# A hybrid encoder block on one core: branch B's values as the stationary operand, and the places around the expert loop rearranged

## The reference, cut to what matters

```python
# branch B: 8 heads of 64, ONE k and ONE v for all heads, k_sel = 128 chosen keys per query
sc = jnp.einsum('bqhd,bqkd->bhqk', q_blk, k_g) * scale - slopes * dist
p = jax.nn.softmax(sc, axis=-1)
y_b = jnp.einsum('bhqk,bqkd->bqhd', p, v_g)
...
merged = g_a * (y_a @ w_branch_a[l]) + g_b * (y_b @ w_branch_b[l])
h = h + merged @ w_out[l]
h = h + memory_cross_attention(rms_norm(h), rms_norm(mem), ...)
...
# experts, E = 32, for the tokens routed to e
hb = silu(xb @ w1[e]) * (xb @ w3[e])      # 1024 -> 512
y += (hb @ w2[e]) * gate                  # 512 -> 1024
...
return rms_norm(h, final_norm)
```

## Time and profile before

| | us |
|---|---|
| three runs | 1073.96, 1075.09, 1076.91 |
| median | 1075.09 |
| the profiled run's own time | 1074.56 |
| its span | 1072.7 |
| PE / DVE / ACT busy in it | 997.1 / 510.8 / 316.6 |

### The profile page before, as it was taken

The page is one execution under the profiler, slowest core; times in us unless marked ns, Lnnn a source line. Parts: engine busy times, 40 slices in busy tenths (PEclk is TensorE's granted clock), DMA queues, the critical chain, the costliest instruction groups (busy, mean ns, idle before and its releaser), DMA issues.

```text
span 1072.7 us, 12319 instructions
## 1 busy us (share of the span) xinstructions
PE 997.1 (93%) x4817; PEld 632.1 (59%) x4817; DVE 510.8 (48%) x923; ACT 316.6 (30%) x589; POOL 38.5 (4%) x58
## 2 busy tenths in 40 slices
PE   5999989999999999999995799999999899899894
PEld 4778857777888888887785344344333333333342
DVE  5269899766437545533337333333333232333335
ACT  6342346665553344443322111111111110001013
POOL 1000000000000000000000100000000000000000
PEclk9999989999999999999997799999999999999997
DMA  7422311212132425521388699999999999999992
GB/s 213 146 79 79 117 41 49 70 40 71 48 118 86 150 83 183 166 79 39 116 322 338 241 427 425 427 427 429 425 425 425 431 424 427 426 427 428 428 384 80
DMA packets 63917, 261.21 MB, mean 244 GB/s; under 512 B 11201, under 2 KB 38898, under 8 KB 49778
## 3 DMA queue, kind: packets, MB, share of 16 engines
q1 hardware_dynamic: 59442, 248.60, 58.5%
q0 software_dynamic: 3104, 7.35, 1.9%
q10 hardware_dynamic: 1312, 4.46, 1.1%
HBM read 260.12 MB, written 4.19 MB: 246 GB/s over the span
## 4 chain that ended last, share of the span: by engine, by line
PE 75%; DMA 13%; DVE 8%; issue 2%; ACT 2%; DVEq 0%; ACTq 0%; POOLq 0%
PE ps L1875 16%; DMA eraw<-in_w 12%; PE ps L1586 12%; PE ps L1588 11%; PE ps L1587 11%; PE ps L1901 8%; PE ps L1912 2%; PE ps L1776 2%; PE ps L1913 2%; PE ps L1755 2%; PE ps L1804 1%; PE ps L1826 1%; PE ps L1763 1%; DVE work L1210 1%; DVE wlo L1175 1%
## 5 line engine op out<-in xcount | busy, mean ns | idle before, releaser
L1875 PE MATMUL ps<-eraw,XT 128*64 128x512 f32 x1024 | 235.8, 604 | 12.5 <-DMA eraw<-in_w 11.7
L1875 PEld LDWEIGHTS ps<-eraw,XT 128*64 128x64 f32 x1024 | 70.5, 138 | 139.6 <-issue 135.7
L1175 DVE TENSOR_TENSOR wlo<-raw,whi 128x2048 fp32r<-128x2048 f32 (+2 forms) x43 | 95.9, 2231 | 108.6 <-ACT whi L879 108.4
L1901 PE MATMUL ps<-eraw,HT 128*64 128x512 f32 x512 | 113.0, 593 | 8.8 <-issue 7.8
L1461 DVE TENSOR_TENSOR h<-ps,h 128x512 f32<-128x512 f32 x128 | 79.4, 683 | 83.4 <-PE ps L1913 83.4
L1586 PE MATMUL ps<-xT_hi,whi 128*128 128x512 f32 (+1 forms) x256 | 104.9, 410 | 3.0 <-DVE xT_lo L1182 2.0
L1587 PE MATMUL ps<-xT_lo,whi 128*128 128x512 f32 (+1 forms) x256 | 101.0, 394 | 0.0
L1588 PE MATMUL ps<-xT_hi,wlo 128*128 128x512 f32 (+1 forms) x256 | 100.8, 394 | 0.0
L879 ACT ACTIVATE whi<-raw 128x2048 fp32r<-128x2048 f32 (+2 forms) x43 | 80.2, 1866 | 45.2 <-PE ps L1588 43.9
L1901 PEld LDWEIGHTS ps<-eraw,HT 128*64 128x64 f32 x512 | 39.9, 137 | 80.1 <-issue 80.1
L1026 ACT ACTIVATE HT<-ps 128x512 f32<-128x512 f32 x16 | 9.6, 598 | 215.5 <-PE ps L1886 215.5
(11 more groups left out here) (304 smaller groups left out, 1539.8 us busy)
## 6 DMA issues: line engine op xcount, KB each, us to landing
eraw<-in_w SPq DMA_DIRECT2D x82, 2048.0 KB, 28.9
eraw<-in_w SPq DMA_DIRECT2D x28, 1024.0 KB, 11.6
raw<-in_w_in SPq DMA_DIRECT2D x9, 1024.0 KB, 5.3
raw<-in_w_gate SPq DMA_DIRECT2D x8, 1024.0 KB, 5.7
raw<-in_w_ckv SPq DMA_DIRECT2D x8, 1024.0 KB, 5.7
raw<-in_w_out SPq DMA_DIRECT2D x4, 1024.0 KB, 5.2
raw<-in_w_cq SPq DMA_DIRECT2D x4, 1024.0 KB, 5.1
raw<-in_w_co SPq DMA_DIRECT2D x4, 1024.0 KB, 5.0
```

Source lines behind the costliest of these rows:

```text
L1175: dve.tensor_tensor(wlo[n % 2][:, 0:w], raw[n % RING][:, 0:w], whi[n % 2][:, 0:w].bitcast(f32), ALU.subtract).then_inc(w_lo, 1)
L1875: ins = pe.matmul(ps[1 + c // 2][rows, :], XT[p % 2][:, kk, rows], eraw[slot][:, first + 512 * k:first + 512 * k + 512], start=(kk == 0), ...
L1901: ins = pe.matmul(ps[4 + n][rows, :], HT[:, ff, rows], eraw[slot][:, first + D * f + 512 * n:first + D * f + 512 * n + 512], start=(ff == ...
```

## The change

- **Branch B.** The roles are exchanged: `vb` (64 columns) is stationary and `pT` (128 columns) moves, the two heads of a unit lie side by side in the two halves of the array, and the result is y transposed. `yb`, its multiplication and the 16 transposes are gone. ACT multiplies the exponentials by the inverted sums ahead of `tr` (two operations a unit), and copies each unit's result to `ybT_hi`; DVE makes `ybT_lo` of it, which now lies in the upper half of h's place. So `h` is loaded behind `mrow`, after the last merge.
- **Around the routing.** `co 3` stands ahead of `hn 1`, and `fT 2`, `fT 3` and `logits 1` ahead of `hn 2`. PE multiplies a constant 3 times behind `rank` and 9 times behind `x_at`, into a bank that nobody reads (`stay_awake`). SP fills the last ring place only when the first gather has landed.
- **The end.** The read of `n_over` stands ahead of each engine's work for the last pair, and ACT's spare root, which brings in the table with roots, behind the branch for `n_over`.

```diff
-    ybT_lo = at("ybT_lo", [P, 4, SEQ], f32r, R_C, 24 * KB)
+    ybT_lo = at("ybT_lo", [P, 4, SEQ], f32r, R_H, 8 * KB)
...
-    yb = at("yb", [P, TT, 512], f32, R_H, 8 * KB)
...
-    steps += [("yT", "b", j) for j in range(4)] + [("split", CH_G[-1] + 2)] + [("sigmoid", i) for i in range(KT // 2)]
+    steps += [("split", CH_G[-1] + 2)] + [("sigmoid", i) for i in range(KT // 2)]
...
-    steps += [("co", 0), ("co", 1), ("fT", 0), ("hn", 0), ("co", 2), ("fT", 1), ("hn", 1), ("co", 3), ("logits", 0),
-              ("hn", 2), ("fT", 2), ("fT", 3), ("logits", 1), ("hn", 3), ("logits", 2), ("logits", 3)]
+    steps += [("co", 0), ("co", 1), ("fT", 0), ("hn", 0), ("co", 2), ("fT", 1), ("co", 3), ("hn", 1), ("logits", 0),
+              ("fT", 2), ("fT", 3), ("logits", 1), ("hn", 2), ("hn", 3), ("logits", 2), ("logits", 3)]
...
             sp.wait_ge(xf_stored, 16 * TT)
+            sp.wait_ge(blk_loaded, 16)
             load_place(NS - 1)
...
-            b, n = use[("yT", "b", 3)]
-            pool.wait_ge(bank_free[b], n + 1)
-            pool.dma_start(h[:, :, :], x[0].rearrange("(t p) n -> p t n", p=P)).then_inc(h_loaded, 16)
             pool.wait_ge(mg_low, len(MERGES))
             pool.dma_start(mrow[:, :, :], mem[0].rearrange("(t p) n -> p t n", p=P)).then_inc(mem_loaded, 16)
+            pool.dma_start(h[:, :, :], x[0].rearrange("(t p) n -> p t n", p=P)).then_inc(h_loaded, 16)
...
+                elif kind == "fin" and UNITS[s[1]][0] == "B":
+                    u = s[1]
+                    qt = UNITS[u][1]
+                    act.wait_ge(sum_inverted, u - len(A_UNITS) + 1)
+                    for m in (0, 1):
+                        b = sbuf[u % 3][m][:, 0:kv(qt)]
+                        ins = act.activation(b, b, ACT.Copy, scale=rsum[:, u % 3, m:m + 1])
+                    ins.then_inc(fin_done, 1)
...
+                    else:
+                        act.activation(ybT_hi[:, j, P * qt:P * qt + P], tile_of(*s)[:, 0:P], ACT.Copy).then_inc(act_hi, 1)
...
-                else:
-
-                    act.activation(sqr[:, 15:16], ident[:, 0:1], ACT.Sqrt)
+            n_over = act.value_load(over_i[0:1, 0:1], min_val=0, max_val=MAX_OVER)
             hidden(NPAIR - 1)
             output(NPAIR - 1)
-            n_over = act.value_load(over_i[0:1, 0:1], min_val=0, max_val=MAX_OVER)
...
+            act.activation(sqr[:, 15:16], ident[:, 0:1], ACT.Sqrt)
...
-                        dve.tensor_tensor(yb[:, qt, P * j:P * j + P].rearrange("p (m n) -> p m n", m=2), p,
-                                          rsum[:, u % 3, 0:2].unsqueeze(2).to_broadcast([P, 2, DH_B]),
-                                          ALU.mult).then_inc(freed(*s), 1)
+                        c = slice(P * qt, P * qt + P)
+                        dve.wait_ge(act_hi, T_NO[s])
+                        dve.tensor_tensor(ybT_lo[:, j, c], tile_of(*s)[:, 0:P], ybT_hi[:, j, c].bitcast(f32),
+                                          ALU.subtract).then_inc(freed(*s), 1)
...
+            n_over = dve.value_load(over_i[0:1, 0:1], min_val=0, max_val=MAX_OVER)
             rest(NPAIR - 1)
-            n_over = dve.value_load(over_i[0:1, 0:1], min_val=0, max_val=MAX_OVER)
...
+            def stay_awake(n):
+
+                for _ in range(n):
+                    pe.matmul(ps[IDLE_BANK][:, 0:256], ident[:, :], gain_o[:, 0:256], start=True, stop=True)
...
+                            for m in (0, 1):
+                                ins = pe.matmul(o[DH_B * m:DH_B * m + DH_B, 0:P], vb[:, k, :], pT[u % 2][m][:, k, :],
+                                                start=(k == 0), stop=(k == qt))
...
-                            for jj in range(4):
-                                copied("yT", "ab"[m], jj)
+                            for jj in range(4 * (1 - m)):
+                                copied("yT", "a", jj)
+                            if m:
+                                copied("av", len(UNITS) - 1)
...
+                    pe.wait_ge(bank_free[IDLE_BANK], bank_uses[IDLE_BANK])
+                    stay_awake(3)
...
                     pair_table(o[:, 0:NE // 2], one_lane, slice(0, P), (by_p, by_tile)).then_inc(full(*s), 1)
+                    stay_awake(9)
```

More of the change, by code:

```diff
@@ L482, in build @@
     max_done, exp_done, fin_done = sem("max_done"), sem("exp_done"), sem("fin_done")
+    sum_inverted = sem("sum_inverted")
     sig_done, mg_sum, mg_high, mg_low = sem("sig_done"), sem("mg_sum"), sem("mg_high"), sem("mg_low")
@@ L516, in build @@
     for s in steps:
-        if s[0] in ("xT", "yT", "mT", "cT"):
+        if s[0] in ("xT", "yT", "mT", "cT") or s[0] == "av" and UNITS[s[1]][0] == "B":
             T_NO[s] = len(T_NO) + 1
@@ L889, in _ @@
                 elif kind == "yT":
[L890 to L893, removed]
-                    else:
-                        act.activation(ybT_hi[:, j, :], p[:, :], ACT.Copy).then_inc(act_hi, 1)
+                    j = s[2]
+                    act.activation(yaT_hi[:, j, :], tile_of(*s)[:, :], ACT.Copy, scale=cols[:, 40:41]).then_inc(act_hi, 1)
                 elif kind == "fT":
@@ L980, in _ @@
                     for g in (2 * s[1], KT + 2 * s[1]):
+                        copied("fm", CH_G[g // 2], 1)
                         v = gates[:, g:g + 2, :].rearrange("p g n -> p (g n)")
@@ L1184, in _ @@
                 elif kind == "yT":
-                    br, j = s[1:]
+                    j = s[2]
                     dve.wait_ge(act_hi, T_NO[s])
[L1187 to L1192, removed]
+                    dve.scalar_tensor_tensor(yaT_lo[:, j, :], tile_of(*s)[:, :], cols[:, 40:41],
+                                             yaT_hi[:, j, :].bitcast(f32), ALU.mult, ALU.subtract).then_inc(freed(*s), 1)
                 elif kind == "index":
@@ L1244, in _ @@
                     else:
-                        dve.reciprocal(rsum[:, u % 3, 0:2], ssum[:, u % 3, 0:2]).then_inc(fin_done, 1)
-                        dve.wait_ge(fin_done, u + 1)
+                        dve.reciprocal(rsum[:, u % 3, 0:2], ssum[:, u % 3, 0:2]).then_inc(sum_inverted, 1)
                 elif kind == "av":
@@ L1599, in pair_table @@
                 return ins
+            IDLE_BANK = [b for b in range(8) if b not in [use[k][0] for k in (("logits",), ("rank",), ("x_at",))]][0]
+            def stay_awake(n):
+                for _ in range(n):
+                    pe.matmul(ps[IDLE_BANK][:, 0:256], ident[:, :], gain_o[:, 0:256], start=True, stop=True)
             for s in steps:
@@ L1645, in _ @@
                 elif kind == "yT":
-                    br, j = s[1:]
-                    if s == ("yT", "b", 0):
-                        copied("av", len(UNITS) - 1)
+                    j = s[2]
                     if s == ("yT", "a", 0):
@@ L1652, in _ @@
                     for t in range(TT):
-                        ins = pe.transpose(o[:, P * t:P * t + P], (ya if br == "a" else yb)[:, t, P * j:P * j + P], ident[:, :])
+                        ins = pe.transpose(o[:, P * t:P * t + P], ya[:, t, P * j:P * j + P], ident[:, :])
                     ins.then_inc(full(*s), 1)
@@ L1773, in _ @@
                         copied("tr", u, m)
-                        for k in range(qt + 1):
-                            v = va[:, k, P * j:P * j + P] if br == "A" else vb[:, k, :]
-                            ins = pe.matmul(o[:, DH_B * m:DH_B * m + (P if br == "A" else DH_B)], pT[u % 2][m][:, k, :], v,
+                    for k in range(qt + 1):
+                        if br == "A":
+                            ins = pe.matmul(o[:, 0:P], pT[u % 2][0][:, k, :], va[:, k, P * j:P * j + P],
                                             start=(k == 0), stop=(k == qt))
+                        else:
+                            for m in (0, 1):
+                                ins = pe.matmul(o[DH_B * m:DH_B * m + DH_B, 0:P], vb[:, k, :], pT[u % 2][m][:, k, :],
+                                                start=(k == 0), stop=(k == qt))
                     ins.then_inc(full(*s), 1)
@@ L1966, in _ @@
                 body(p)
+            n_over = pe.value_load(over_i[0:1, 0:1], min_val=0, max_val=MAX_OVER)
             turn_hidden(NPAIR - 1)
@@ L1969, in _ @@
             down(NPAIR - 1, 5)
-            n_over = pe.value_load(over_i[0:1, 0:1], min_val=0, max_val=MAX_OVER)
             with pe.If(n_over > 0):
```

2 lines of the change are left out of this document (removed).

## The result

The changed kernel takes 1070.22 us (median of 5, 1067.96 to 1070.46) where the kernel before, on the same chip, took 1074.84. The ratio is 0.9947, with a 95% interval of 0.9933 to 0.9961: 0.5% faster, 4.6 us by the medians and 5.7 by the ratio. The forecast was 1063.6 with a range of 1057 to 1069. The direction was right, the size was about half, and the measured time lies outside the range. The profiled execution took 1070.22 (span 1068.5).

A forecast was written before the change was run, and what follows sets the result against it. PE sets the pace in branch B, the full transfer engines in the loop, restarting on PE's first release. 2.6 + 2.3 - 1.2 + 1.5 + 4.2 + 2.1 = 11.5 off 1074.6: 1063.1 profiled, 1063.6 by median; range 1057 to 1069.

The forecast's parts named there:

- Products of branch B: Branch B: products in two halves of the array gain 2.6 us over 16 units; ends 8.4 and -5.8.
- rival 2: Branch B: heads don't overlap, or ACT stalls PE in every round; 1072.0 at worst, 1068 for half; chance 0.14.
- rival 4: Branch B: weight loads of the halves go one after the other, making it slower, 1077.1; chance 0.04.
- Rival 1: Branch B: no drain on such small products, or hidden behind loads; products give 8.4, time 1057.8; chance 0.16.
- Transposes of yb: Before the merge: DVE's 0.30 and PE's 1.97 leave the chain, a gain of 2.3 us.
- ACT's new work: Branch B: two multiplications a unit and copies take ACT from 55.5 to about 72 us; loss 1.2, ends 0 and 4.
- h behind mrow: Load of h issued behind mrow lands by about 364, before DVE's first read at 367.05; effect 0.
- Order round the logits: Around the logits: PE ends earlier with copies ahead of `hn 2`, DVE then bounds; gain 1.5 us (0.5 to 1.9).
- The loop's beginning: Start of the loop: shorter gather, transposes and first 32 instructions without cold clock; gain 4.2 us, ends 1.5 and 5.
- Rivals 3 and 5: Loop's beginning: constant products too long or clock left low, 1067 to 1070, chance 0.10; change does nothing there, 1067.8, 0.04.
- The end: Kernel's end: table load gone (1.28) and read of `n_over` moved ahead (0.8); gain 2.1 us, ends 1.2 and 2.2.

The follow-up runs named there:

- c2: Changed kernel with the probabilities' scaling on DVE and ya's norm taken apart (mean, root behind exponentials, then inverse and product): 1062.6 us, ratio 0.9869.
- e12: Changed kernel with the order of the logits and the rows of hn as before: 1071.97 us, ratio 0.9966.
- e1: Kernel before with all edits except those of branch B and the loading of h: 1068.5 us, ratio 0.9935.
- e9: Changed kernel with the end as before (ACT's root table load and the `n_over` reads undone): 1071.98 us, ratio 0.9962.
- e8: Kernel before with branch B's edits alone, h behind mrow included: 1077.27 us, ratio 1.0008.
- e4: Changed kernel with the last ring place loaded without waiting for the gather: 1075.27 us, ratio 0.9999.
- e10: Changed kernel with the scaling of branch B's probabilities moved from ACT to DVE: 1064.14 us, ratio 0.9899.
- e13: Changed kernel with ya's norm taken apart, the scaling of the probabilities left on ACT: 1066.51 us, ratio 0.9904.

## Why the forecast was too large

By its own steps:

1. *Products of branch B*: right in mechanism, and a little too small. Forecast for one unit of tile 0, 1, 2 and 3, with the way in and out: 0.57, 0.79, 1.0, 1.22. Measured: 0.38, 0.59, 0.81, 1.02, and 0.14 on the transposes behind: 0.52, 0.73, 0.95, 1.16. Over 16 units that is a gain of 3.5 where 2.6 was forecast. Both halves' overlap (rival 2's first half) and serial loads (rival 4) are settled: they overlap. Rival 1 (8.4, no cost of switching; its end stands as 1057.7 and as 1057.8) falls, since the switches cost nearly what was forecast.
2. *Transposes of yb*: as forecast, 2.3 (0.30 and 1.97 are gone, the merge follows the values). Steps 1 and 2 make 5.8; c2's branch B is 6.2 shorter than before.
3. ***ACT's new work* is the step that failed.** "I take a loss of 1.2 in all; ends 0 and 4." It cost 7.2 us: branch B is 104.3 long where c2, with the same products, has 97.1. Of this 5.3 are waits and about 1.9 the clock. ACT's total was forecast well (72, measured 72.4). I looked at unit 20, saw that ACT's two multiplications would stand between DVE's inversion and PE, and charged their length (0.8, measured 0.91). I didn't follow what the multiplication itself waits for: the inversion, queued behind DVE's 2.07 us product of ya, which waits for ACT's root, with a table load on each side of it. In the kernel before, DVE's inversion stood behind that product too, but ACT could go on with the exponentials; now ACT stands in its order and everything behind it is late too. And the inversion itself comes 1.2 us later against PE's values, since the new copy stands ahead of the first table load. The bound of 4 took 0.25 a round as if the loss were spread; it fell in one place, and the clock came down with it, of which the text says nothing. That the text named the place and still bounded it by the length of the added instructions is the error.
4. *h behind mrow*: as forecast, 0. It was issued at 355.9, landed 10.8 us later, and DVE read it first at 368.9, 2.2 us after that where 3 were forecast.
5. *Order round the logits*: -1.5 forecast, -2.0 measured (e12).
6. *The loop's beginning*: -4.2 forecast; e1 less e12's and e9's parts leaves 3.4. The pieces are near the forecast (gather 3.28 for 3.2; transposes 1.15 for 0.88, so that 0.8 is won there and not 1.1; first 32 instructions 7.09 for 7.2; constant products ending at 593.8 for 594.4), but the constant products bring 1.3 at the end and not 2.7, since the late ring place fills the gap anyway, and the gather starts later than it could for the stores of xf. Rivals 3 and 5 fall with it.
7. *The end*: -2.1 forecast, -1.6 measured (e9). From the last wait for weights to the end it is 64.4 us, and 66 in the kernel before and in e9. DVE's part came out (its additions start 0.9 sooner behind PE's last `down`), the table load's did not in full: without the 1.28, ACT's second square waits 0.38 for DVE's additions, and DVE's mean, which had lain under the load, stands in the chain.

The measured parts, 0.9 for branch B (e8) and -7.0 for the rest (e1), make -6.1 beside the 5.7 measured for the whole. What the chances left out is rival 2 in its right form: not a stall in every round, but one, where two chains in ACT's order meet.

## What to carry to other kernels

When work is moved to an engine that has room on the mean, ask first what the moved instruction waits for, and what stands behind it in that engine's order; a loss in one place can be several times the length of the instructions added, and here it brought the matmul clock down with it. Put a table-switching operation where its input is long there, and leave what others wait for ahead of a long bulk operation (c2: mean early, root straight behind exponentials, product last). Where a latency-bound gather shares the transfer engines with a stream, release them by different events, and count each microsecond in which the stream stands still.

## What the runs showed of the hardware

- Switching between full width and halves: 16 products in halves take 1.02 us, 0.064 each; the eight transposes behind them are 0.14 longer than the earlier trace rows (1.02 for 0.88). The page TensorEngine Tiling (Array Packing) of the Trainium skill says, in its section Tiling Modes, that a switch of mode drains the engine. The trace agrees, and puts this drain at 0.14 us for small products, less than the 0.2 read in the earlier trace rows.
- The same gather takes 3.28 us beside idle transfer engines, 4.18 beside the end of a load, and 7.72 when it is issued together with a 2 MB ring place (e4). A store of 512 KB behind the ring's loads takes 10.89.
- The granted clock fell to 1.2 GHz at 238 to 239, after PE had been busy for 0.27 of 2 us, and was back at 2.4 GHz at 246. In e10 PE was busy for 0.86 of the 2 us from 236 on, and the clock stood at 0.50 from 238 to 241. In e13 PE was busy for 2.10 of the 3 us from 245 on, and the clock stayed at 1.00.
